# Which rows go into the first block: two tiles and the sample, then three and three, in a kernel of one transformer layer with an expert lookup

## The reference

```python
xn = rmsnorm(x, norm1_g)
z = xn @ w_in                       # conv B, C, h | q, k, v | two gates
u = cg * hh; y = sum(conv_w[j] * up[:, j:j + T] for j in range(3)); conv_y = bg * y
p = softmax(q k^T / 8)              # two components a head, 8 heads
o = (p[0] - lam * p[1]) @ v         # then a norm per head
mix = gates[0] * (conv_y @ w_conv_out) + gates[1] * (o @ w_attn_out)
x = x + mix @ w_o
# expert lookup: 8 heads, the best 16 of 128 x 128 pairs of keys for each row
q = rmsnorm(xn2 @ wq); s_top, i_top = top_k(q . subkeys, 16)
best, sel = top_k(all sums of pairs, 16); g = softmax(best)
h = gelu(u[e] . xn2); x = x + sum over the 128 experts e of g * h * v[e]
```

## Time and profile before

| | us |
|---|---|
| median of 3 runs | 3828.57 (3826.69 to 3834.05) |
| the profiled execution's own time | 3828.75 |
| its span, first to last instruction | 3826.9 |
| first dot product begins | 594.0 |

### The profile page before, as it was taken

The page is one execution under the profiler, slowest core; times in us unless marked ns, Lnnn a source line. Parts: engine busy times, 40 slices in busy tenths (PEclk is TensorE's granted clock), DMA queues, the critical chain, the costliest instruction groups (busy, mean ns, idle before and its releaser), DMA issues.

```text
span 3826.9 us, 46601 instructions
## 1 busy us (share of the span) xinstructions
PE 3148.4 (82%) x14585; PEld 1448.0 (38%) x14585; DVE 2519.1 (66%) x5860; ACT 1457.2 (38%) x4439; POOL 1497.4 (39%) x1411
## 2 busy tenths in 40 slices
PE   7999998788988999796888887778888866666666
PEld 4555555344434554352334342445424411111111
DVE  4332018888888864678777777886566965656664
ACT  3222002356662243323456555224433333333333
POOL 2110003355654432424545464443343343344442
PEclk9999999899988999897889898889998966666666
DMA  5223338799999999989999999999999999999998
GB/s 184 92 84 112 99 132 325 276 387 389 417 391 404 418 417 380 413 334 368 413 341 401 353 375 382 374 417 416 418 416 419 396 404 419 420 420 419 411 420 339
DMA packets 252390, 1338.62 MB, mean 350 GB/s; under 512 B 27280, under 2 KB 65968, under 8 KB 116720
## 3 DMA queue, kind: packets, MB, share of 16 engines
q0 software_dynamic: 152400, 1108.54, 71.1%
q1 hardware_dynamic: 94032, 214.18, 15.3%
q10 hardware_dynamic: 5712, 12.91, 0.9%
HBM read 1309.44 MB, written 26.10 MB: 349 GB/s over the span
## 4 chain that ended last, share of the span: by engine, by line
PE 46%; DMA 22%; DVE 16%; ACT 7%; issue 4%; DVEq 2%; ACTq 1%; POOL 1%; POOLq 0%
DMA mix<-in_peer_uv,tl_idx 11%; DMA ringx<-in_peer_uv,tl_idx 10%; PE tl_ps L1077 9%; PE tl_ps L983 9%; PE tl_ps L816 7%; PE tl_ps L1060 4%; PE tl_ps L964 3%; PE tl_ps L996 3%; PE tl_ps L881 3%; DVE ringx L1783 3%; DVE mix L1783 3%; PE tl_ps L791 2%; DVE xa L1795 2%; PE tl_ps L850 2%; DMA mix<-in_peer_uv,tl_itop 1%
## 5 line engine op out<-in xcount | busy, mean ns | idle before, releaser
L737 POOL DMA_INDIRECT ringx<-in_peer_uv,tl_idx x568 | 675.0, 1188 | 878.5 <-PE tl_ps L1077 589.6
L1077 PE MATMUL tl_ps<-ringx,tl_dg 64*64 64x512 f32 x3808 | 650.8, 770 | 292.2 <-ACT tl_dg L1332 287.4
L1783 DVE CUSTOM_DVE_ANT_0 ringx<-ringx,xb 128x1024 f32<-128x1024 f32 x585 | 708.6, 1221 | 277.2 <-DMA ringx<-in_peer_uv,tl_idx 246.1
L737 POOL DMA_INDIRECT mix<-in_peer_uv,tl_idx x456 | 543.3, 1191 | 827.1 <-PE tl_ps L1077 484.0
L1321 ACT ACTIVATE tl_hg<-tl_hd 128x1 f32<-128x1 f32 x1056 | 213.3, 202 | 1417.6 <-DVE tl_hd L1783 1406.1
L1783 DVE CUSTOM_DVE_ANT_0 mix<-mix,xb 128x1024 f32<-128x1024 f32 x471 | 571.1, 1222 | 244.5 <-DMA mix<-in_peer_uv,tl_idx 218.5
L1077 PE MATMUL tl_ps<-mix,tl_dg 64*64 64x512 f32 x2832 | 471.9, 749 | 231.7 <-ACT tl_dg L1332 227.4
L983 PE MATMUL tl_ps<-tl_xr,low 128*128 128x384 f32 (+1 forms) x1280 | 399.0, 466 | 8.3 <-DVE tl_xr L1709 8.3
L1077 PEld LDWEIGHTS tl_ps<-ringx,tl_dg 64*64 64x64 f32 x3808 | 120.4, 155 | 671.9 <-ACT tl_dg L1332 573.7
L1325 ACT ACTIVATE tl_hw<-tl_hg,tl_gw 128x1 f32<-128x1 f32 x1024 | 301.5, 294 | 74.8 <-issue 5.7
L983 PEld LDWEIGHTS tl_ps<-tl_xr,low 128*128 128x128 f32 x1280 | 242.7, 194 | 182.2 <-issue 53.1
(11 more groups left out here) (221 smaller groups left out, 3888.7 us busy)
## 6 DMA issues: line engine op xcount, KB each, us to landing
low<-in_wall SPq DMA_DIRECT2D x240, 512.0 KB, 7.8
low<-in_watt SPq DMA_DIRECT2D x60, 512.0 KB, 9.1
ringx<-in_peer_uv,tl_idx POOLq DMA_INDIRECT x568, 14.3
mix<-in_peer_uv,tl_idx POOLq DMA_INDIRECT x456, 13.7
ringx<-in_watt SPq DMA_DIRECT2D x12, 512.0 KB, 6.4
u<-in_x_prompt SPq DMA_DIRECT2D x8, 512.0 KB, 12.2
out_y_prompt<-xa ACTq DMA_DIRECT2D x16, 256.0 KB, 8.6
tl_xr<-in_ck_t SPq DMA_DIRECT2D x8, 512.0 KB, 7.9
```

Source lines behind the costliest of these rows:

```text
L737: nc.gpsimd.indirect_dma_start(out=ring[q % RING].rearrange("p a d -> p (a d)"), out_offset=None, in_=A["peer_uv"], in_offset=bass.Indirec ...
L1077: last = nc.tensor.matmul(ps[half_of(h), b, :], dg[rows, npe(q) % DIAGS, :], ring[q % RING][rows, 1, h * 512:(h + 1) * 512], start=k == 0, ...
L1783: nc.vector.tensor_tensor_reduce(out=ring[q % RING][:, 0, :], in0=ring[q % RING][:, 0, :], in1=xb[:, t % 2, :], scale=1.0, scalar=0.0, op0 ...
```

## The change

The sample moves from block 2 to block 0, tiles 2 and 5 move one block on: block 0 is tiles 0, 1 and the sample (288 columns in place of 384), block 1 tiles 2, 3, 4, block 2 tiles 5, 6, 7 (384 in place of 288). The slots stay in the order of the tiles, with the sample last. So block 1 has to be through before slot 256 and block 2 before slot 640. `place` maps a tile to its block and place. The cached keys and values now come in the prologue, into the ring buffers that the lookup does not use yet, and SyncE issues them between the conv loads. Earlier keys are 256 for block 1 (384 before) and 640 for block 2 (768 before), both double-buffered. In block 0's attention the sample's scores take the banks 2 to 4, so conv C must have been copied out of bank 3 first, and conv B goes to bank 5. The conv step of block 0 treats rows and sample as two segments, as block 2 did. The sample's indices and weights are made in units 6 and 7, at slots 148 and 172, and kept in tables of their own. `ATT`, `PLAN`, `SHARED` and `UNIT_AT` have new numbers. The load of the next tile's row is put at slot 116 of a tile, not 64, where the next tile is of another block.

```diff
-BLOCKS = ((0, 3 * P, (0, 1, 2)), (3 * P, 3 * P, (3, 4, 5)), (6 * P, 2 * P + DEC, (6, 7, 8)))
+BLOCKS = ((0, 2 * P + DEC, (0, 1, 8)), (2 * P, 3 * P, (2, 3, 4)), (5 * P, 3 * P, (5, 6, 7)))
+LONGEST = 5 * P
...
-ATT = ((-330, 1.0), (29.5, 0.75), (366, 0.93))
+ATT = ((-330, 1.0), (35.2, 0.5), (255, 0.9))
...
-PLAN = ((-106.5, 1600, 1600, 7), (176.5, 1, 1750, 7), (549, 1, 1100, 7))
+PLAN = ((-100.8, 1600, 1585, 8.3), (134.7, 1, 2800, 5), (437.9, 1, 1750, 7.6))
...
-SHARED = ((0,170,1,6),(170,300,3,4),(336,520,1,6),(520,680,2,3))
+SHARED = ((0, 123, 0, 6), (124, 235, 4, 3), (255, 425, 1, 5), (425, 600, 1, 2))
...
-UNITS = [(0, h, 2) for h in range(0, PH, 2)] + [(t, h, 4) for t in range(1, NT + 1) for h in (0, 4)]
-UNIT_AT = ((-3.1, 0.2), (11.1, 1), (19.9, 1), (28.5, 1), (40, 3), (68, 3), (130, 4), (170, 5), (325, 3), (350, 3),
-           (394, 4), (450, 5), (514, 5), (560, 5), (742, 3), (774, 4), (850, 4), (900, 4), (950, 4), (985, 4))
+UNITS = [(0, h, 2) for h in range(0, PH, 2)] + [(t, h, 4) for t in (1, NT, 2, 3, 4, 5, 6, 7) for h in (0, 4)]
+UNIT_AT = ((-3.1, 0), (16.8, 1), (25.6, 1), (34.2, 1), (45.7, 3), (87.7, 3), (148.0, 4), (172, 3), (231, 3.3), (260, 4), (300, 5.1), (344.7, 5), (400, 3.7), (443.8, 5.2), (590, 4.9), (622, 5), (660, 4.5), (718.5, 5), (788.5, 5.3), (838.5, 5))
...
+def place(t):
+
+    return (0, 2) if t == NT else (0, t) if t < 2 else (1 + (t - 2) // 3, (t - 2) % 3)
...
-        vc = parts(u1, 7904, DC, P)
...
-        kTp, vp, kTc = behind[:, 0:768], parts(behind, 768, 6, P), behind[:, 1536:2560]
+        kTp, vp = parts(behind, 0, 2, LONGEST), parts(behind, 2 * LONGEST, 2 * LONGEST // P, P)
+        CACHE = (NT + 1) * 4 * HD + 3 * D
+        kTc, vc = ringx[:, CACHE:CACHE + PAST], parts(ringx, CACHE + PAST, DC, P)
+        sidx, sgw = sb("sidx", [P, DEC], U32), sb("sgw", [P, DEC])
...
                         store_heads(h)
-                        for k in range(3):
-                            load_conv(h + 1, k)
+                        load_conv(h + 1, 0)
+                        load_conv(h + 1, 1)
+                        load_cache_keys(h + 1)
+                        load_conv(h + 1, 2)
+                        load_cache_values(h + 1)
...
                         if t == NT:
-                            pe.wait_ge(s["kc_in"], 16 * (g - 2 * DC + 1))
+                            pe.wait_ge(s["kc_in"], 16 * (g + 1))
+                            pe.wait_ge(s["c_done"], g + 1)
...
                             if k == 2:
-                                pe.wait_ge(s["c_done"], cc + 1)
+                                pe.wait_ge(s["u_done"], cc + 1)
                             elif cc:
-                                pe.wait_ge(s["u_done" if k else "y_done"], cc)
+                                pe.wait_ge(s["y_done" if k else "c_done"], cc)
                         w = low_block(keep, 3 + k).rearrange("p (c n) -> p c n", c=DC)
-                        last = nc.tensor.matmul(ps[:, (3, 5, 3)[k], 0:nr], w[:, c, :], xn[:, c, 0:nr], start=(c == 0), stop=(c == DC - 1))
+                        last = nc.tensor.matmul(ps[:, (3, 5, 5)[k], 0:nr], w[:, c, :], xn[:, c, 0:nr], start=(c == 0), stop=(c == DC - 1))
...
-                if k == 64 and t < NT:
+                if t < NT and k == (64 if t + 1 == NT or place(t + 1)[0] == place(t)[0] else 116):
                     load_row(t + 1)
...
+                    if (t, h0) == (NT, 4):
+                        for quad in [slice(p * DEC, (p + 1) * DEC) for p in range(P // DEC)]:
+                            nc.vector.tensor_copy(sidx[quad], idx[quad, 2, quad])
+                            nc.vector.tensor_copy(sgw[quad], gw[quad, 2, quad])
+                        nc.vector.drain().then_inc(s["s_ready"], 1)
```

More of the change, by code:

```diff
@@ L106, in build_norm1 @@
         block = ctx.enter_context(nc.Block())
+        rows = [P, P, DEC]
         @block.sync
@@ L110, in _ @@
             for b in range(FIRST):
-                sp.dma_start(xt[:, b, :], A["x_prompt"][0, b * P:(b + 1) * P, :]).then_inc(x_in[b], 16)
+                src = A["x_prompt"][0, b * P:(b + 1) * P, :] if b < 2 else A["x_sample"][0]
+                sp.dma_start(xt[:rows[b], b, :], src).then_inc(x_in[b], 16)
                 if b == 0:
@@ L452, in first_gate @@
             if t == NT:
-                return NU + 1 if k == 0 else 0
+                return 0
             return UNITS.index((t, k // TOPK, 2 if t == 0 else 4)) + 1 if k % (32 if t == 0 else 64) == 0 else 0
         def table(own, spread, t):
-            return own[:, t % 2] if t < NT else spread[:, 0, 0:DEC // TOPK].rearrange("p a b -> p (a b)")
+            return own[:, t % 2] if t < NT else spread
         @block.sync
@@ L522, in store_heads @@
                 cols = slice(h * P, (h + 1) * P)
-                full = 3 if rb < 2 else 2
+                full = 3 if rb else 2
                 sp.wait_ge(s["qf_d"], 3 * (g + 1))
@@ L1416, in sum_pairs @@
             def sum_pairs(t, h0, nh):
-                both = tops[:, t % 3, 2 * h0:2 * (h0 + nh), :].rearrange("p (h c) k -> p h c k", c=2)
+                both = tops[:, place(t)[1], 2 * h0:2 * (h0 + nh), :].rearrange("p (h c) k -> p h c k", c=2)
                 for first, i0, i1, wide in PAIRS:
@@ L1474, in indices @@
                 slots = slice(h0 * TOPK, (h0 + nh) * TOPK)
-                nc.vector.scalar_tensor_tensor(out=idx[:, t % 2, slots], in0=e01[:, 0, 0:nh].rearrange("p h k -> p (h k)"),
+                nc.vector.scalar_tensor_tensor(out=idx[:, 2 if t == NT else t % 2, slots], in0=e01[:, 0, 0:nh].rearrange("p h k -> p (h k)"),
                                                scalar=float(NKEYS), in1=e01[:, 1, 0:nh].rearrange("p h k -> p (h k)"),
@@ L1501, in weights_end @@
                 dve.drain()
-                nc.vector.tensor_tensor(gw[:, t % 2, slots].rearrange("p (h k) -> p h k", h=nh), best[:, 0:nh],
+                nc.vector.tensor_tensor(gw[:, 2 if t == NT else t % 2, slots].rearrange("p (h k) -> p h k", h=nh), best[:, 0:nh],
                                         gs[:, 0:nh].unsqueeze(2).to_broadcast([P, nh, TOPK]), ALU.mult)
@@ L1507, in routing @@
                 for u, (t, h0, nh) in enumerate(UNITS):
-                    ends = plan(t // 3)[1] + [plan(t // 3)[1][-1] + 2]
+                    rb = place(t)[0]
+                    ends = plan(rb)[1] + [plan(rb)[1][-1] + 2]
                     assert u == 0 or unit_at(u, 0) >= ends[40 + 2 * (h0 + nh)] + 1
-                    assert t > 5 or unit_at(u, nh + 4) < plan(t // 3 + 1)[1][41]
+                    assert rb == 2 or unit_at(u, nh + 4) < plan(rb + 1)[1][41]
                     heads = range(nh)
@@ L1642, in attend @@
+                    last.then_inc(s["y_done"], 1)
                 for u in range(-3, 3 * DC + 1):
@@ L1686, in middle @@
                     nc.vector.tensor_copy(U[:, 0:2], ut[:, cc, :])
-                    if len(segs) == 2:
-                        nc.vector.tensor_copy(U[:, m + 2:m + 4], st[:, cc, :])
                     dve.wait_ge(s["c_done"], DC * rb + cc + 1)
                     dve.wait_ge(s["z_done"], BASE[rb] + 3 * cc + 2)
-                    for a, b, shift in segs:
-                        last = nc.vector.tensor_tensor(U[:, 2 + a + shift:2 + b + shift], ps[:, banks + 1, a:b], Cb[:, a:b], ALU.mult)
@@ L1706, in middle @@
+                    nc.vector.tensor_copy(ut[:, cc, :] if rb == 1 else ends_out[:, 0:2, cc], U[:, n:n + 2])
                     dve.drain()
                     dve.wait_ge(s["z_done"], BASE[rb] + 3 * cc + 3)
-                    for a, b, shift in segs:
-                        last = nc.vector.tensor_tensor(cvT[:, cc, a:b], ps[:, banks + 2, a:b], Y[:, a + shift:b + shift], ALU.mult)
-                    last.then_inc(s["y_done"], 1)
+                    nc.vector.tensor_tensor(cvT[:, cc, 0:n], ps[:, banks + 2, 0:n], Y[:, 0:n], ALU.mult).then_inc(s["y_done"], 1)
```

177 lines of the change are left out of this document (84 added, 93 removed).

## The result

The changed kernel takes **3926.83 us** (median of 4 runs, 3920.97 to 3930.20) against 3830.93 for the kernel before in the same runs: a ratio of 1.0247, 95% interval 1.0234 to 1.0259. It is slower by 96 us; 3,905 had been forecast, 3,800 to 4,000 as the range. The profiled execution took 3930.2 us with a span of 3928.4, so it stands 101.5 us over the span of before.

The account below looks back on a forecast made before the run. Memory nearly always full beside dense work, with TensorE also full in block 1's middle part; stages summed to 3,329 us after a first dot at 574, a span of 3,903, plus 1.9 around it: 3,905 us, range 3,800 to 4,000.

Parts of the forecast that it names:

- The main step: Whole stream: the same dense work beside 150 slots fewer, which then run alone at 2.53 us each; a loss of 96 us.
- signs that would have shown it wrong: DMA staying above 390 GB/s between 700 and 1,700 us, or the slots left at the end not running at 2.53 us.
- the rest: End of the stream, no dense work beside it: 456 slots at 2.53 us, 1,154 us.
- Middle 1: Block 1's middle part: TensorE sets it and can be full, 345 us for 70 slots, DMA at 310 to 320 GB/s.
- attention 2: Block 2's attention: memory 481 to 516 us, TensorE 452, the sample's wait gone; put at 510 us.
- Attention 1: Block 1's attention, 95 slots: TensorE 317 us, memory 309, VectorE about 275, three near limits; put at 332 us.
- TensorE with 5% of gaps: Block 1's attention: the allowance for idle TensorE that took its sum of 317 us to 332 us.
- Rival C: Attention of blocks 1 and 2 held by the chain between engines within a tile, 18.2 and 23.3 us each: 4,059 us; chance 0.14.
- The prologue: Before the first dot: -41 middle part, -31 conv, +50 sample's attention, +2 last head, sum -20; first dot at 574 us.
- D: Prologue: the sample eats the whole gain, first gather no earlier; 3,925 us, inside the range, no chance of its own.
- The short stretches between the stages: Gaps between the stream's stages: 61 slots in 166 us.
- B: Engines overlap without waiting, each stage takes only its largest engine sum, prologue reaches 555: 3,817 us or some 3,790; chance 0.20.

Follow-up runs that it names:

- a_thin: Changed kernel with the matmuls over every second contraction chunk left out in block 1's conv and merge blocks (part of the computation missing): 3860.9 us.
- b_thin: Kernel before with the matmuls over every second contraction chunk left out in block 1's conv and merge blocks (part of the computation missing): 3817.81 us.
- b_early1: Kernel before, blocks not regrouped, with only block 1's pace (attention, middle part, VectorE shares, early units) set as in the changed kernel: 3968.52 us, ratio 1.0359.
- a_split: Changed kernel with the sample's second scores moved from ahead of the projection to between its fourth and fifth chunk: 3896.86 us, ratio 1.0180.
- a_share: Changed kernel with one slot in six of slots 4 to 123 summed by VectorE in place of TensorE: 3930.30 us, ratio 1.0255.

## Why the prediction was right, and where it was off

**The main step held.** "The dense work does not shrink, it is done in 150 slots fewer, and those slots then run alone at 2.53 us": 147 slots at 2.535 us. a_thin and b_thin show that TensorE sets block 1's middle part now, where memory had set it as well, and b_early1 that the pace alone brings such a loss without any regrouping. Of the signs that would have shown it wrong neither came: DMA was at 302 to 355 GB/s in the stages up to 1,603 us, and the rest ran at 2.535 us a slot.

**The stages of the stream.** Middle 1 was put at 345 us and took 342, queries 1 at 125 and took 125, attention 2 at 510 and took 510, middle 2 at 412 and took 415, queries 2 at 135 and took 139, block 0's queries at 138 and took 136.5, the rest at 1,154 and took 1,146. Where one engine or memory is full, its sum over the rows of before gives the stage to within 1 to 3%. DMA in middle 1 was put at 310 to 320 GB/s and was 330.

**Attention 1 was mis-sized**: 332 us forecast, 363 measured. The step "TensorE with 5% of gaps" failed: TensorE's sum was right (317 forecast, 322 measured), but its gaps were 11% (41 of 363). The experiments show waits between engines in them that move from one link to another when one is removed, and a stage that still grows with TensorE's work. Rival C held here in that part only, at 15.1 us a tile and not 18.2.

**The prologue was mis-sized**: the first dot at 574 forecast, 595.5 measured, which is D. The columns scaled as said: the 32 weight blocks took 124.4 us in place of 165.4 (41.0 for 41.3 forecast). The sample's attention was put at 6.3 us a head and took 8.0: heads now begin 44.2 us apart in place of 40.1, with 3.9 us less for the conv. The wait was 2.3 us and not 1.7, and behind it came 1.5 us of half clock that the sum did not have. The last head was put at 8.3 and cost about twice that: from its first projection to the middle part it takes 62.9 us in place of 50.3, with the conv's 3.9 us gone there too; what sets it was not tried. Attention from its first projection to the middle part took 376.0 us (16.8 to 392.8) where it had taken 335.5, so 40.5 more, and with the 31 us of the conv that is 71.5 where 52 stood. So the prologue's gain of 72 us was eaten up.

**Errors that cancelled.** The short stretches between the stages took 143 us in place of 166 (52 slots lie in them, not 61), and the rest 8 less. Against them stand +21.5 and +31. The sum of 3,903 came to 3,928.4, and without the cancelling it would have been 56 us off. That the time lies 22 us from the forecast is in part luck, and so is the closeness to rival D's 3,925: D named the prologue rightly (the sample eats the whole gain), but it left out attention 1, which the two errors the other way made up for.

**The rivals.** B (all engines overlap) did not occur: attention 1 and the prologue both went the other way. D occurred. C had its price in neither attention: 363 us and not 436, 510 and not 560.

## What to carry to other kernels

Where a stream bound by memory runs beside dense work, a slot that loses its cover costs its whole memory time at the end, and the stage that it leaves gives back less as long as something else sets that stage. Here 147 slots cost 373 us and gave back 272. So count the slots that have cover before and after, price the difference at the bare rate, and set against it what the covered stages get shorter; the work itself can stay as it is. A wait that costs nothing beside a full memory costs its length in a prologue, and the clock behind it on top, so move such work only with something to fill it. A planner's single number of slack between two engines (here the sums behind the dots) is worth trying before the order of the work is rebuilt: it gave 0.6% where the rebuild lost 2.5%.

## What the runs showed of the hardware that was not expected

TensorE, busy for 552 of the 594 us of the same stage in the kernel before and for 534 of 595 here, fell to half clock after a single idle time of 2.28 us, some 2 us after it had come back: the weight loads of the next projection stand 0.64 us apart, then 0.32, and the projection takes 6.97 us in place of 5.43. With the gap filled by a_split it takes 2.77 + 2.70. The Trainium skill (TensorE: Matmul & The Clock Gate, HAM oscillation) describes such a fall behind idle gaps and the loss with it, and the trace agrees in kind; the gaps of the page's case are waits for transfers and longer than the 2.28 us here. A head so loses 1.5 us in clock on top of 2.3 us of idleness, 3.8 in all; a_split gave back 3.5 to 3.9 us in each of the seven heads that it reaches.

A second thing: work taken off TensorE came off its busy time only in part, and the granted clock fell each time. In a_share the sums of 15 slots left TensorE in block 1's attention (120 matmul records fewer in the rows above), some 16 us at the 1.07 us of the prediction, and its busy time fell by 9 us only, at a granted clock of 0.92 in place of 0.94. In a_thin and b_thin 144 us of work brought 129 and 110 us, at 0.93 and 0.87 in place of 1.00 and 0.99. That the slower clock took the rest fits these rows; it was not tried by itself.
